# Retention rounds: two small matmul groups move out of the middle of their products

## The reference, cut to what matters

```
xn = rmsnorm(h); u = xn @ w_in      # last columns of u: the gates ga, gb (1024 each)
# retention, chunk by chunk, per head:
scores = (q k^T) * decay
o      = scores v + (q * q_decay) r
r_new  = chunk_decay * r + (k * k_decay)^T v
a_ret  = head_rmsnorm(o) * silu(rg)
mixed  = sigmoid(ga) * y_hg + sigmoid(gb) * y_ret ;  h = h + mixed @ w_out
```

## Time and profile before

| | |
|---|---|
| median of 3 runs | 919.84 us (919.07 to 920.59) |
| profiled execution | 919.76 us, its span 917.9 us |
| PE busy | 906.6 us, 99% of the span |
| DVE, ACT, POOL busy | 533.6, 370.9, 238.2 us |
| mean granted TensorE clock | 0.996 |

### The profile page before, as it was taken

The page is one execution under the profiler, slowest core; times in us unless marked ns, Lnnn a source line. Parts: engine busy times, 40 slices in busy tenths (PEclk is TensorE's granted clock), DMA queues, the critical chain, the costliest instruction groups (busy, mean ns, idle before and its releaser), DMA issues.

```text
span 917.9 us, 21087 instructions
## 1 busy us (share of the span) xinstructions
PE 906.6 (99%) x8016; PEld 895.8 (98%) x8016; DVE 533.6 (58%) x651; ACT 370.9 (40%) x511; POOL 238.2 (26%) x289
## 2 busy tenths in 40 slices
PE   9999999999999999999999999999999999999995
PEld 8999999999999999999999999999999999999995
DVE  6432278888765565665576666666666433435654
ACT  7323446646554555223343333333333222213433
POOL 0006087787111100004621111111111121213431
PEclk9999999999999999999999999999999999999998
DMA  7332533233245443633323333333333333332312
GB/s 227 100 93 86 184 94 99 61 92 102 70 129 157 116 130 107 194 119 101 92 70 94 91 91 91 91 91 91 91 91 109 96 94 94 94 92 68 106 34 94
DMA packets 176473, 94.75 MB, mean 103 GB/s; under 512 B 17888, under 2 KB 174960, under 8 KB 176016
## 3 DMA queue, kind: packets, MB, share of 16 engines
q1 hardware_dynamic: 149698, 80.61, 29.5%
q10 hardware_dynamic: 26736, 13.60, 5.4%
HBM read 86.25 MB, written 8.03 MB: 103 GB/s over the span
## 4 chain that ended last, share of the span: by engine, by line
PE 97%; DVE 1%; DMA 1%; ACT 0%; issue 0%; ACTq 0%; SPq 0%; DVEq 0%
PE acc L497 87%; PE lvb L635 1%; DMA xtok<-in_x_prompt 1%; PE lvb L497 1%; PE mb L745 0%; PE ob L671 0%; PE lvb L528 0%; PE lvb L631 0%; PE ob L724 0%; PE mb L728 0%; PE ob L723 0%; PE lvb L709 0%; PE ob L666 0%; PE lvb L581 0%; DVE sfull L1373 0%; PE lvb L833 0%
## 5 line engine op out<-in xcount | busy, mean ns | idle before, releaser
L889 ACT ACTIVATE whi<-raw 128x1024 fp32r<-128x1024 f32 (+2 forms) x132 | 146.8, 1112 | 364.8 <-PE acc L497 363.9
L1254 DVE TENSOR_TENSOR wlo<-raw,whi 128x1024 fp32r<-128x1024 f32 (+2 forms) x131 | 197.7, 1509 | 154.0 <-ACT whi L889 154.0
L497 PE MATMUL acc<-xah,whi 128*128 128x260 f32 x896 | 185.5, 288 | 0.2
L497 PE MATMUL acc<-xah,wlo 128*128 128x260 f32 x896 | 180.3, 283 | 0.0
L497 PE MATMUL acc<-xal,whi 128*128 128x260 f32 x896 | 179.9, 282 | 0.0
L497 PE MATMUL acc<-xbh,whi 128*128 128x260 f32 x816 | 165.0, 283 | 0.0
L497 PE MATMUL acc<-xbh,wlo 128*128 128x260 f32 x816 | 164.4, 283 | 0.0
L497 PE MATMUL acc<-xbl,whi 128*128 128x260 f32 x816 | 164.1, 283 | 0.0
L497 PEld LDWEIGHTS acc<-xah,whi 128*128 128x128 f32 x896 | 137.9, 188 | 2.3
L497 PEld LDWEIGHTS acc<-xah,wlo 128*128 128x128 f32 x896 | 137.9, 188 | 0.0
L497 PEld LDWEIGHTS acc<-xal,whi 128*128 128x128 f32 x896 | 137.9, 188 | 0.0
(11 more groups left out here) (307 smaller groups left out, 1172.5 us busy)
## 6 DMA issues: line engine op xcount, KB each, us to landing
raw<-in_w_in SPq DMA_DIRECT2D x96, 256.0 KB, 3.1
raw<-in_w_up SPq DMA_DIRECT2D x88, 256.0 KB, 3.1
raw<-in_w_down SPq DMA_DIRECT2D x16, 384.0 KB, 3.3
raw<-in_w_down SPq DMA_DIRECT2D x16, 320.0 KB, 3.7
raw<-in_w_out SPq DMA_DIRECT2D x16, 256.0 KB, 2.9
raw<-in_w_ple_gate SPq DMA_DIRECT2D x8, 512.0 KB, 3.7
x_transposed<-xstg SPq DMA_DIRECT2D x1, 2080.0 KB, 7.9
hT<-x_transposed ACTq DMA_DIRECT2D x1, 2080.0 KB, 8.8
```

Of the source, the lines that this page charges most:

```text
L497: mm = pe.matmul(sums[:, b, 0:HT], wt[slot][:, w], xx[:, c, b * HT:(b + 1) * HT], start=first and i == 0 and q == 0, stop=last and i == n ...
L889: act.activation(whi[k % 2][:, 0:n], raw[k % 2][:, 0:n], ACT.Copy).then_inc(hi_ready, 1)
L1254: dve.tensor_tensor(wlo[k % 2][:, 0:n], raw[k % 2][:, 0:n], whi[k % 2][:, 0:n].bitcast(fp), SUB).then_inc(lo_ready, 1)
```

## The change

In rounds 0, 1 and 2 the third and fourth products (k = 2 and 3) are no longer cut in two. The head squares come behind the whole third product, directly ahead of the sample dots, and the sample squares come behind the whole fourth product, directly ahead of the next round's product 0. The last round is written out by itself behind the loop and keeps the order of before. The sample dots go to the bank `lvb` 0 with semaphores of their own (`rdots_full`, `rdots_free`), so that `mb` has three fillings in a round. ScalarE and VectorE follow the order of TensorE: in rounds 0 to 2 the root of the head means comes behind gate 2 and the root of the sample means, with the copies behind it, behind gate 3; on VectorE the dots' copy and squares and the `wlo` of product 2 come ahead of `gate_outputs`, and the sample gates come behind the `wlo` of product 3. ScalarE's order as a list, for rounds 0 to 2:

- before: `kst`, `vst`, rsm DMA, whi/gate 0, vb DMA, whi/gate 1, squares, head root, out DMA, whi/gate 2, sample root, `arh`, `smp` copies, whi/gate 3
- after: `kst`, `vst`, rsm DMA, whi/gate 0, vb DMA, whi/gate 1, squares, out DMA, whi/gate 2, head root, whi/gate 3, sample root, `arh`, `smp` copies

The core of the diff (left out: the counts of `misc_full` and `misc_free` that follow from three fillings instead of four, and the body of VectorE's `sample_gates`, which is unchanged):

```diff
-            with pe.Fori(0, 4) as it:
+            def retention_chunk(it, last=False):
                 product("C", 0, it, 0, 0, C8, 0, xah, xal)
                 pe.wait_ge(staged, it * 2 + 1)
                 pe.wait_ge(vst_ready, it + 5)
                 wait_level(L_C, 0, it, 2)
+
+                pe.wait_ge(rdots_free, it + 1)
...
-                product("C", 2, it, 0, 2, range(4), 0, xah, xal, last=False)
-                pe.wait_ge(sq_ready, it + 5)
-                wait_misc(M_C, 1, it, 4)
-                pe.wait_ge(sums_ready, 1)
-                pe.matmul(mb[:], ones128r[:], sqh[:], start=True, stop=False)
-                pe.matmul(mb[:], ones128r[:], sql[:], start=False, stop=True).then_inc(misc_full, 1)
-                product("C", 2, it, 0, 2, range(4, 8), 4, xah, xal, first=False, wait_unit=False)
-                wait_misc(M_C, 2, it, 4)
-                pe.wait_ge(smp_staged, it + 5)
-                pe.wait_ge(rsm_ready, it + 1)
-                for b in range(NS):
-                    for r in range(2):
-                        rows = slice(64 * r, 64 * r + 64)
-                        mm = pe.matmul(mb[rows, b:b + 1], rsm[:, b, rows], qs8[:, b:b + 1], start=True, stop=True)
-                mm.then_inc(misc_full, 1)
...
-                product("C", 3, it, 1, 3, range(4), 0, xah, xal, last=False)
-
-                pe.wait_ge(smp_sq, it + 1)
-                wait_misc(M_C, 3, it, 4)
-                pe.matmul(mb[:, 0:8], blk64, sqs[:, 0:8], start=True, stop=True)
-                pe.matmul(mb[:, 8:16], ones128[:], sqs[:, 8:16], start=True, stop=True).then_inc(misc_full, 1)
-                product("C", 3, it, 1, 3, range(4, 8), 4, xah, xal, first=False, wait_unit=False)
+                def head_squares():
+                    pe.wait_ge(sq_ready, it + 5)
+                    wait_misc(M_C, 1, it, 3)
+                    pe.wait_ge(sums_ready, 1)
+                    pe.matmul(mb[:], ones128r[:], sqh[:], start=True, stop=False)
+                    pe.matmul(mb[:], ones128r[:], sql[:], start=False, stop=True).then_inc(misc_full, 1)
+
+                def sample_dots():
+                    pe.wait_ge(smp_staged, it + 5)
+                    pe.wait_ge(rsm_ready, it + 1)
+                    for b in range(NS):
+                        for r in range(2):
+                            rows = slice(64 * r, 64 * r + 64)
+                            mm = pe.matmul(lvb[rows, 0, b:b + 1], rsm[:, b, rows], qs8[:, b:b + 1], start=True, stop=True)
+                    mm.then_inc(rdots_full, 1)
+
+                def sample_squares():
+                    pe.wait_ge(smp_sq, it + 1)
+                    wait_misc(M_C, 2, it, 3)
+                    pe.matmul(mb[:, 0:8], blk64, sqs[:, 0:8], start=True, stop=True)
+                    pe.matmul(mb[:, 8:16], ones128[:], sqs[:, 8:16], start=True, stop=True).then_inc(misc_full, 1)
+
+                def whole_or_halves(k, group):
+
+                    if last:
+                        product("C", k, it, k % 2, k, range(4), 0, xah, xal, last=False)
+                        group()
+                        product("C", k, it, k % 2, k, range(4, 8), 4, xah, xal, first=False, wait_unit=False)
+                    else:
+                        product("C", k, it, k % 2, k, C8, 0, xah, xal)
+                        group()
+
+                whole_or_halves(2, head_squares)
+                sample_dots()
+                whole_or_halves(3, sample_squares)
+
+            pe.sem_inc(rdots_full, 1)
+            with pe.Fori(0, 3) as it:
+                retention_chunk(it)
+            retention_chunk(3, last=True)
...
-            with act.Fori(0, 4) as it:
-                act.wait_ge(misc_full, it * 4 + (M_C - 3))
+            def retention_chunk(it, last=False):
+                act.wait_ge(misc_full, it * 3 + (M_C - 2))
                 taken()
                 act.activation(kst[:], chunk(kr, it), ACT.Copy)
                 act.activation(vst[:], vr[:, it, :], ACT.Copy).then_inc(vst_ready, 1)
                 act.wait_ge(rsm_stored, it * 16 + 16)
-                act.wait_ge(misc_full, it * 4 + M_C)
+                act.wait_ge(rdots_full, it + 1)
                 taken()
                 act.dma_start(rsm[:], state_ret[0].rearrange("b h d v -> h d b v")[it]).then_inc(rsm_loaded, 16)
-                for k in range(4):
-                    if k == 3:
-                        act.wait_ge(misc_full, it * 4 + (M_C + 4))
-                        act.activation(rss[:], mb[:, 0:16], ACT.Sqrt, bias=eps[:]).then_inc(misc_free, 1)
-                        branch_hi(arh, it, 4)
-                        act.wait_ge(smp_done, it + 1)
-                        taken()
-                        for i, t in enumerate((ahh, arh)):
-                            act.activation(t[:, it, NT:TT], smp[:, i], ACT.Copy).then_inc(smp_hi, 1)
...
+                def weights(k):
                     done("C", k, it)
-                    ahead("C", k, it)
+                    ahead("C", k, it, "D" if last else None)
+
+                def gate(k):
                     act.activation(two(gab[:, it * 2 + (k // 2 + DC * (k % 2)), :]), ps2(k),
                                    ACT.Sigmoid).then_inc(acc_free[k % 2], 1)
-                    if k == 0:
-                        act.wait_ge(vs_stored, 32)
-                        act.dma_start(vb[:].rearrange("k (b v) -> k b v", b=NS),
-                                      vs_dram[1, :, bass.ds(it * 128, 128)].unsqueeze(0)
-                                      .broadcast_to([128, NS, 128])).then_inc(vb_loaded, 32)
-                    if k == 1:
-                        act.wait_ge(ret_o, it + 1)
-                        act.activation(sq[:], ob[:], ACT.Square).then_inc(sq_full, 1)
-                        act.wait_ge(sq_full, it + 5)
-                        taken()
-                        act.activation(sqh[:], sq[:], ACT.Copy).then_inc(sq_hi, 1)
-                        act.wait_ge(misc_full, it * 4 + (M_C + 2))
-                        act.activation(rs[:], mb[:], ACT.Sqrt, bias=eps[:]).then_inc(misc_free, 1)
-                        act.wait_ge(rsm_ready, it + 1)
-                        taken()
-                        act.dma_start(ret_sample[0].rearrange("b h d v -> h d b v")[it], rsm[:])\
-                            .then_inc(rsm_stored, 16)
...
+                def head_roots():
+                    act.wait_ge(misc_full, it * 3 + (M_C + 2))
+                    act.activation(rs[:], mb[:], ACT.Sqrt, bias=eps[:]).then_inc(misc_free, 1)
+
+                def sample_roots():
+                    act.wait_ge(misc_full, it * 3 + (M_C + 3))
+                    act.activation(rss[:], mb[:, 0:16], ACT.Sqrt, bias=eps[:]).then_inc(misc_free, 1)
+                    branch_hi(arh, it, 4)
+                    act.wait_ge(smp_done, it + 1)
+                    taken()
+                    for i, t in enumerate((ahh, arh)):
+                        act.activation(t[:, it, NT:TT], smp[:, i], ACT.Copy).then_inc(smp_hi, 1)
+
+                weights(0)
+                gate(0)
+                act.wait_ge(vs_stored, 32)
+                act.dma_start(vb[:].rearrange("k (b v) -> k b v", b=NS),
+                              vs_dram[1, :, bass.ds(it * 128, 128)].unsqueeze(0)
+                              .broadcast_to([128, NS, 128])).then_inc(vb_loaded, 32)
+                weights(1)
+                gate(1)
+                act.wait_ge(ret_o, it + 1)
+                act.activation(sq[:], ob[:], ACT.Square).then_inc(sq_full, 1)
+                act.wait_ge(sq_full, it + 5)
+                taken()
+                act.activation(sqh[:], sq[:], ACT.Copy).then_inc(sq_hi, 1)
+                if last:
+                    head_roots()
+                act.wait_ge(rsm_ready, it + 1)
+                taken()
+                act.dma_start(ret_sample[0].rearrange("b h d v -> h d b v")[it], rsm[:])\
+                    .then_inc(rsm_stored, 16)
+                weights(2)
+                gate(2)
+                if last:
+                    sample_roots()
+                else:
+                    head_roots()
+                weights(3)
+                gate(3)
+                if not last:
+                    sample_roots()
+
+            act.wait_ge(misc_full, M_C)
+            taken()
+            with act.Fori(0, 3) as it:
+                retention_chunk(it)
+            retention_chunk(3, last=True)
...
-                dve.wait_ge(misc_free, it * 4 + (M_C + 2))
-                gate_outputs(grt, it, 4, per=3)
-                dve.wait_ge(misc_full, it * 4 + (M_C + 3))
-                taken()
-                dve.tensor_copy(qr[:, it, NT:TT], mb[:, 0:NS]).then_inc(misc_free, 1)
-
-                dve.wait_ge(misc_free, it * 4 + (M_C + 3))
-                taken()
-                done("C", 2, it)
-                ahead("C", 2, it)
-                dve.wait_ge(misc_free, it * 4 + (M_C + 4))
-                step(dve.reciprocal(rss[:], rss[:]))
...
```

(87 more changed lines are left out.)

## The result

The changed kernel is slower: 939.07 us (median of 4 runs, 938.75 to 939.63) against 919.58 (4 runs, 919.07 to 920.59), ratio 1.0207 [1.0195, 1.022]. The sign is as predicted, the loss of 19.5 us is more than double the 8.7 of the sum, and the time lies outside the range (924.9 to 932). The profiled execution's span is 937.0 us, before 917.9: 19.1 us more.

What follows compares the result with a forecast made beforehand. TensorE, with 97% of the span, bounds the kernel; late `vst` makes the scores wait at three transitions, 3 x 2.9 = 8.7 us, less 0 to 0.6 for uncut products. 919.8 + 8.7 = 928.5 us, range 924.9 to 932.

Steps and rivals of the forecast that it cites:

- the sum: Whole kernel: three transitions at 2.9 us each, 8.7 us, less 0 to 0.6 us, added to 919.8 us.
- what bounds and where it stalls: TensorE has 97% of the span; scores of rounds 1 to 3 wait 2.5 to 3.1 us each for ScalarE's `vst`.
- what the uncut products are worth: TensorE, rounds 0 to 2: costed at nothing, bounds 0 and a gain of 0.1 us per cut, 0.6 in all.
- What it moves on ScalarE: Chain from product 3's end through gate 3 and sample root to `vst`: 9.05 us, making the scores wait 2.9 us.
- the step from the two copies to `kst`: ScalarE, next round's start: 0.25 us for the `smp` copies plus 0.4 for the loop's edge, bounds 0 and 0.6.
- the predicted lower bound: TensorE's wait ahead of the scores at one transition: 2.5 us, the low end around 2.9.
- the clock as a rival: TensorE's clock falls in the waits before the scores, slowing matmuls behind them: 7 us more, 935.5 us; chance 0.11.
- its 5.8 us: Clock rival: the TensorE stretch behind each wait that could take up to twice as long, bounds 0 and 4.6 us.
- The collision of the sample gates: Rival: VectorE's sample gates no longer collide with GpSimd's `qst`; chain 1.2 us shorter, 924.9 us; chance 0.07.
- A drain at each table switch: Rival on ScalarE: two switches per chain cost 2.76 us more at each of three transitions, 936.8 us; chance 0.03.
- The other side: Rival at `kst` of rounds 1 to 3: ScalarE is in time, chain under 6.2 us, 919.4 us; chance 0.03.
- no change: Rival: ScalarE misses the scores by less than 0.6 us each, 920 to 921.5 us; chance 0.03.

## Why the prediction was right or wrong

**Right: what bounds and where it stalls.** The idle is where the prediction puts it, ahead of the scores and released by `vst`, at three transitions, and the reason is the program order on ScalarE: putting the copies ahead of the sample root takes 16 of the 19.5 us away.

**Right: what the uncut products are worth.** Costed at nothing, at most 0.6 us. Rounds without stalls take 29.10 us against 29.12, and the time is the same.

**Right up to the sample root.** It ends the wait for gate 3 and two loads 4.49 us behind product 3 (277.29 to 281.78); the prediction has 4.53. The copies of `smp` come 7.53 us behind product 3 in round 0, but 7.30 and 7.27 in rounds 1 and 2, against 7.25. So 0.25 us are of the first round only, in ScalarE's wait for `smp` (2.24, then 2.01 and 1.99); why, stays open. Also as the prediction has it, the edge costs 0.40 us behind two short copies, and nothing is late at the dots.

**Wrong: "What it moves on ScalarE", the step from the two copies to `kst`, and with it the sum's 3 x 2.9.** The step counts the copies and 0.4 for the edge. The loop's head got a table load of 1.28 us as well. I had followed the loads ahead of gate and root, but not asked which table the loop is entered with and which it ends with. `kst` comes 9.53 and 9.28 us behind product 3 in rounds 0 and 1 instead of 7.9. The idle is 4.56 and 4.31 us in rounds 1 and 2. In the last, behind the loop and without a load and an edge, it is 2.52, the predicted lower bound. The same load delays round 0 by 0.84 us, which the prediction calls "as before". Together 12.2 us of idle where the sum has 8.7. With the load alone removed from rounds 1 and 2, the first transition has the predicted chain to 0.1 us.

**Wrong: the clock as a rival at 0.11.** It is no rival but a consequence, and it came at all three waits. Its price, 3 x 2.3 = 7, was near the measured 6.1 to 6.5 us, though by luck in part: no row gives its 5.8 us, and twice as long for 5.8 would be 5.8 more and not 4.6; measured are 5.5, 3.4 and 3.4 us at half speed. Its chance was not near. The reason for it was weak: that small matmuls preceded the one fall that the trace of before shows. The Trainium skill (TensorE: Matmul & The Clock Gate, section HAM oscillation) has the clock fall in idle gaps between bursts. The trace agrees in that each fall had such a gap ahead of it, of 4.56, 4.31 and 2.52 us, but only the first lay within its gap; the other two came as the scores began and 0.6 us behind that. With waits close to the predicted 2.9 us (2.97, 2.94 and 2.89) it fell at two of three.

Either omission alone breaks the range, whose upper end is 932: with the clock held and the load in place the time is 932.57, with the load gone from rounds 1 and 2 and the clock falling twice it is 934.08 (some 1 us of it the wait that the added Sqrt makes in round 0).

**The other rivals.** The collision of the sample gates did not go away: the two multiplications still take 0.47 and 1.05 us. A drain at each table switch is not seen either: `kst` starts 0.02 us behind the end of its load (285.52 + 1.28 to 286.82). The other side and "no change" fell with the waits.

**Left open.** Between 2.2 and 3.2 us of idle its length does not tell whether the clock falls: it fell with 2.97, 2.89, 2.52, 2.45 and 2.35 us, and held with 3.15, 2.94, 2.34 and 2.22. Behind the waits of 1.1 us or less it always held. That the load at the loop's head is the compiler's answer to two different tables at one place fits all eight kernels run with this loop (a load in the five whose entry and end differ, none in the three where they agree), but the compiler itself was not looked at.

## What to carry to other kernels

When an instruction is moved to the end of a loop's round, follow what stands behind it over the edge into the next round, on every engine, and check on ScalarE that the loop is entered and left with the same table. Where TensorE is dense, price a wait of 2 us or more twice, the idle and the slower matmuls behind it. And when one late producer is mended, look for the next: here `kst`, then `qst`, then VectorE's work beside `vb`.

## What the hardware showed that was not expected

- A table load of 1.28 us stood ahead of a Copy at the head of a loop that is entered on one table and ends on another. The Copy itself needs none: in the last round it starts 0.22 us behind the instruction ahead of it.
- The grant of 0.50 outlasts the wait: in round 1 until 293.7, 5.5 us after TensorE had begun again. Of the seven falls in these traces two, with waits of 4.56 and 2.97 us, came clearly while TensorE was idle; the others came just as it began again or up to 0.9 us later. A fall costs 1.6 to 2.7 us here: scores to outputs take 8.74 to 9.89 us against 7.1 to 7.2 behind a wait without a fall.
- Two equal waits in one kernel, 2.97 and 2.94 us, had scores of 2.07 and 1.15 us behind them.
- A two-input subtraction on VectorE (1.23 us) takes 2.93 when a multiplication on GpSimd (1.90) starts 0.05 us ahead of it, nearly the two one after the other (3.1). With a start 0.38 us behind it takes 2.60. The order counts: with `kst` and `vst` ahead of the root the subtraction comes first (350.96) and keeps its 1.23, and the multiplication (351.28) takes 2.66. The Trainium skill (SBUF — State Buffer, section Who interferes with whom) says that a VectorE instruction with two SBUF inputs and a GpSimd instruction that reads SBUF exclude each other, the later one waiting; the trace agrees.
